# Latent attention: where the inverse sums are spread and the outputs scaled and split, in a two-layer transformer kernel

## The reference, cut to what matters

```python
for l in range(DEPTH):
    h = rms_norm(x, g_mix[l])
    proj = h @ w_in[l]
    c_q, c_kv, k_r, qkv_b, qkv_c, gate_logits = jnp.split(proj, IN_SPLITS, axis=-1)
    y_a = mla_mixer(c_q, c_kv, k_r, g_q[l], g_kv[l], w_uq[l], w_ukv[l])
    ...
    y_b = dilated_mixer(q_b, k_b, qkv_b[:, :, 2])
    y_c = neighbourhood_mixer(qkv_c[:, :, 0], qkv_c[:, :, 1], qkv_c[:, :, 2], rpb[l])
    ...
    merged = (gates[:, :, 0] * (y_a @ w_pa[l]) + gates[:, :, 1] * (y_b @ w_pb[l])
              + gates[:, :, 2] * (y_c @ w_pc[l]))
    x = x + merged @ w_o[l]
    ...

def attend(blk):        # in mla_mixer, 8 heads
    qn, qr = blk
    s = (jnp.einsum('bqhd,bkhd->bhqk', qn, k_nope) + jnp.einsum('bqhr,bkr->bhqk', qr, k_rope)) * scale
    p = jax.nn.softmax(s, axis=-1).astype(v.dtype)
    return jnp.einsum('bhqk,bkhd->bqhd', p, v)
```

## Time and profile before

| | before |
|---|---|
| median of 3 timed executions | 3363.31 us (3362.96 to 3364.73) |
| the profiled execution | 3372.84 us, its span 3371.0 us |
| TensorE busy (matmuls) | 3314.4 us, 98% |
| VectorE busy | 1596.5 us, 47% |
| ScalarE busy | 1244.7 us, 37% |
| GpSimd busy | 353.3 us, 10% |
| TensorE's share of the chain that ended last | 91% |

### The profile page before, as it was taken

The page is one execution under the profiler, slowest core; times in us unless marked ns, Lnnn a source line. Parts: engine busy times, 40 slices in busy tenths (PEclk is TensorE's granted clock), DMA queues, the critical chain, the costliest instruction groups (busy, mean ns, idle before and its releaser), DMA issues.

```text
span 3371.0 us, 39038 instructions
## 1 busy us (share of the span) xinstructions
PE 3314.4 (98%) x15780; PEld 2709.2 (80%) x15780; DVE 1596.5 (47%) x2314; ACT 1244.7 (37%) x2007; POOL 353.3 (10%) x321
## 2 busy tenths in 40 slices
PE   8999999999999999999999999999999999999998
PEld 7885788888887867888888877878888888888887
DVE  5465444443445573445343544334433349754244
ACT  4564323322335553224322332222322247742222
POOL 3121000100011220001000111002200032230001
PEclk9999999999999998999999999999999999999999
DMA  4121223222222211232222232222222222322222
GB/s 154 57 82 41 69 94 100 94 94 100 94 95 76 78 50 42 88 100 94 94 100 94 94 103 78 91 85 69 88 96 98 95 81 89 100 82 94 100 98 71
DMA packets 83234, 295.26 MB, mean 88 GB/s; under 512 B 9616, under 2 KB 12016, under 8 KB 82928
## 3 DMA queue, kind: packets, MB, share of 16 engines
q1 hardware_dynamic: 80352, 283.78, 25.4%
q0 software_dynamic: 2704, 8.98, 0.8%
HBM read 289.55 MB, written 3.18 MB: 87 GB/s over the span
## 4 chain that ended last, share of the span: by engine, by line
PE 91%; DVE 3%; ACT 2%; POOL 2%; issue 2%; DMA 0%; SPq 0%; DVEq 0%; ACTq 0%; POOLq 0%
PE bank L2504 27%; PE bank L2506 27%; PE bank L2505 27%; PE bank L2753 2%; PE bank L2761 2%; PE bank L2784 1%; PE bank L2896 1%; DVE w_lo L1872 1%; ACT w_hi L1420 1%; POOL xs L1210 1%; PE bank L2723 1%; PE bank L2585 1%; PE bank L2886 1%; PE bank L2646 0%; PE bank L2595 0%
## 5 line engine op out<-in xcount | busy, mean ns | idle before, releaser
L1872 DVE TENSOR_TENSOR w_lo<-raw_ring,w_hi 128x1024 fp32r<-128x1024 f32 x530 | 666.8, 1259 | 1155.8 <-ACT w_hi L1420 1155.1
L2504 PE MATMUL bank<-h_hi,w_hi 128*128 128x512 f32 (+1 forms) x2752 | 1065.5, 387 | 15.5 <-DVE w_lo L1872 10.6
L2506 PE MATMUL bank<-h_hi,w_lo 128*128 128x512 f32 (+1 forms) x2752 | 1054.6, 383 | 0.0
L2505 PE MATMUL bank<-h_lo,w_hi 128*128 128x512 f32 (+1 forms) x2752 | 1054.5, 383 | 0.0
L1420 ACT ACTIVATE w_hi<-raw_ring 128x1024 fp32r<-128x1024 f32 x530 | 560.6, 1058 | 1168.9 <-PE bank L2506 1095.8
L2504 PEld LDWEIGHTS bank<-h_hi,w_hi 128*128 128x128 f32 x2752 | 520.2, 189 | 120.2 <-issue 15.0
L2506 PEld LDWEIGHTS bank<-h_hi,w_lo 128*128 128x128 f32 x2752 | 519.6, 189 | 102.2
L2505 PEld LDWEIGHTS bank<-h_lo,w_hi 128*128 128x128 f32 x2752 | 520.3, 189 | 100.2 <-issue 1.5
L2504 PE MATMUL bank<-act_hi,w_hi 128*128 128x512 f32 (+1 forms) x1336 | 507.6, 380 | 2.1 <-ACT arena L1440 1.2
L2506 PE MATMUL bank<-act_hi,w_lo 128*128 128x512 f32 (+1 forms) x1336 | 504.7, 378 | 0.0
L2505 PE MATMUL bank<-act_lo,w_hi 128*128 128x512 f32 (+1 forms) x1336 | 504.5, 378 | 0.0
(11 more groups left out here) (211 smaller groups left out, 2652.0 us busy)
## 6 DMA issues: line engine op xcount, KB each, us to landing
raw_ring<-weights SPq DMA_DIRECT2D x530, 512.0 KB, 3.3
arena<-rpb POOLq DMA_DIRECT2D x16, 320.0 KB, 3.6
xs<-x_t SPq DMA_DIRECT2D x8, 256.0 KB, 6.5
out_t<-xs SPq DMA_DIRECT2D x16, 128.0 KB, 1.8
arena<-block SPq DMA_DIRECT2D x1, 1024.0 KB, 9.0
arena<-o_nat POOLq DMA_DIRECT2D x2, 512.0 KB, 3.4
arena<-ret POOLq DMA_DIRECT2D x4, 256.0 KB, 3.2
o_nat<-arena POOLq DMA_DIRECT2D x2, 384.0 KB, 3.1
```

Source lines behind the costliest of these rows:

```text
L1872: nc.vector.tensor_tensor(w_slot(w_lo, u), raw_slot(u), f32(w_slot(w_hi, u)), ALU.subtract) \
L2504: nc.tensor.matmul(out, lhs[0], rhs[0], start=first, stop=False)
L2505: nc.tensor.matmul(out, lhs[0], rhs[1], start=False, stop=False)
L2506: return nc.tensor.matmul(out, lhs[1], rhs[0], start=False, stop=last)
```

## The change

It does five things.

- The generator of a latent group yields R no longer together with O, but with four new kinds of step from a table, `LATENT_ENDS`: E (reciprocal and spread), R, Y (the multiplication) and H and L (high and low part of the split). E of the first output is in step j = 6 in place of 4, R in step 7; batch 0 of the next dense part holds Y of the first; batch 1 H of the first and E of the second; batch 2 L of the first and R of the second.
- Y, H and L of the second output come later still: for A0 in steps 1, 2 and 3 of A1's main part, behind that step's transposes (`LATENT_LAST`), for A1 behind projections 3, 4 and 5 of C1 (`LATENT_DENSE`). `turned` does nothing for A any more.
- V of a latent group asks `before` only for the units in which V's own weights lie (`units_of`), no more all that have a free slot. The others come with the pairs of heads (`split_ahead`).
- In the dense part of a group with rotation VectorE does `turned` ahead of the last weight split and the last rotation (B0 is the one group that this concerns).
- The plan of banks and the order of splits follow.

```diff
-TURNS = {("B", 0): [("C", 0)], ("A", 1): [("B", 2), ("A", 0)], ("C", 1): [("A", 1)]}
+TURNS = {("B", 0): [("C", 0)], ("A", 1): [("B", 2)]}
...
+LATENT_ENDS = {6: [("E", 3)], 7: [("R", 3)], 8: [("Y", 3)], 9: [("H", 3), ("E", 7)], 10: [("L", 3), ("R", 7)]}
+LATENT_LAST = {1: "Y", 2: "H", 3: "L"}
+LATENT_DENSE = {3: "Y", 4: "H", 5: "L"}
...
         if br == "A":
-            ends = j >= LATENT_LAG_O and ends_head(br, g, j - LATENT_LAG_O)
-            if ends:
+            if j >= LATENT_LAG_O and ends_head(br, g, j - LATENT_LAG_O):
                 yield "O", j - LATENT_LAG_O
             if LATENT_LAG_T <= j < n + LATENT_LAG_T:
                 yield "T", j - LATENT_LAG_T
-            if ends:
-                yield "R", j - LATENT_LAG_O
+            if g and part == "main" and j in LATENT_LAST:
+                yield LATENT_LAST[j], -1
+            if j in LATENT_ENDS:
+                yield from LATENT_ENDS[j]
             continue
...
+        def units_of(key):
+
+            return piece_at[weight_pieces(key)[-1]][0] + 1
...
+            def latent_end(l, kind, g, two):
+                if kind == "H":
+                    wait_freed(act, (l, "A", g, "O", two))
+                    hi((l, "yt", "A", g, two), part(act_hi, YT_TILE["A", g] + two), latent_out(two))
...
+                            key = (l, "v", br, g, t)
+                            if br == "A":
+                                before(key, units_of(key) - split[0])
...
+            def latent_end(l, kind, g, two):
+                y = latent_out(two)
+                if kind == "E":
+                    both = slice(2 * NT * two, 2 * NT * (two + 1))
+                    wait_freed(dve, (l, "A", g, "S", 2 * NT * (two + 1) - 1))
+                    then(nc.vector.reciprocal(row_inv[:, both], latent_sum[:, both]))
+                    if g:
+                        dve.wait_ge(lo_ready, lo_at[l, "yt", "A", 0, two])
+                    else:
+                        dve.wait_ge(mixed_b, l + 1)
+                    inv = row_inv[:, both].rearrange("p (s t o) -> p t s o", s=2, o=1)
+                    nc.vector.tensor_copy(y.rearrange("p (t s d) -> p t s d", t=NT, s=2),
+                                          inv.to_broadcast([P, NT, 2, HEAD])).then_inc(latent_inv, 1)
+                elif kind == "Y":
+                    key = (l, "A", g, "O", two)
+                    wait_acc(dve, key)
+                    wait_freed(dve, (l, "A", g, "R", two))
+                    nc.vector.tensor_tensor(y, bank(key)[:, :], y, ALU.mult).then_inc(latent_freed, 1)
+                elif kind == "L":
+                    i = YT_TILE["A", g] + two
+                    lo((l, "yt", "A", g, two), part(act_lo, i), y, part(act_hi, i))
...
+                        if (br, g) == ("C", 1) and m in LATENT_DENSE:
+                            latent_end(l, LATENT_DENSE[m], 1, 1)
...
+                    for group_ in TURNS.get((br, g), []):
+                        turned(l, group_)
                     if has_rope(br) and n_dense(br, g) == 5:
                         before((l, "v", br, g, 0))
                         rotate(l, br, g, 4)
-                    for group_ in TURNS.get((br, g), []):
-                        turned(l, group_)
```

More of the change, by code:

```diff
@@ L531, in turned @@
         def turned(group):
-            for f in range(0 if group[0] == "A" else 2):
+            for f in range(2):
                 p.add((l, "yt") + group + (f,), "dve")
@@ L550, in attend @@
                         p.add((l, "vt" if turns_v(br, g) else "v", br, g, t), "act")
+                    continue
+                if kind in "EYHL":
                     continue
@@ L664, in split_order @@
         out.extend((("h", "q", l, k), True) for k in range(2))
-        for br, g in GROUPS:
-            if (br, g) in YT_TILE:
-                out.extend(((l, "yt", br, g, f), br == "A") for f in range(2))
+        for br, g, f in SPLIT_TURNED:
+            out.append(((l, "yt", br, g, f), br == "A"))
         out.extend((("merged", l, m), True) for m in range(KD))
@@ L1593, in turned @@
                     key = (l, "yt") + group + (f,)
-                    if group[0] == "A":
-                        wait_freed(act, (l,) + group + ("O", f))
-                        hi(key, part(act_hi, YT_TILE[group] + f), latent_out(f))
-                        continue
                     before(key)
@@ L2149, in turned @@
             def turned(l, group_):
-                if group_[0] == "A":
-                    for two in range(2):
-                        key = (l,) + group_ + ("O", two)
-                        wait_acc(dve, key)
-                        wait_freed(dve, (l,) + group_ + ("R", two))
-                        y = latent_out(two)
-                        nc.vector.tensor_tensor(y, bank(key)[:, :], y, ALU.mult).then_inc(latent_freed, 1)
-                    for f in range(2):
-                        i = YT_TILE[group_] + f
-                        lo((l, "yt") + group_ + (f,), part(act_lo, i), latent_out(f), part(act_hi, i))
-                    return
                 for f in range(2):
@@ L2168, in attend @@
                     if kind == "V":
-                        if not turns_v(br, g):
+                        if br == "A":
+                            key = (l, "v", br, g, v_tiles(j)[-1])
+                            before(key, units_of(key) - split[0])
+                        elif not turns_v(br, g):
                             before((l, "v", br, g, v_tiles(j)[-1]))
+                        continue
+                    if kind in "EYHL":
+                        latent_end(l, kind, *latent_pair(g, j))
                         continue
@@ L2183, in attend @@
                             nc.vector.tensor_copy(pt_tile(br, u)[:, 0:w], b[:, 0:w]).then_inc(dve_freed, 1)
-                            if br == "A" and ends_head(br, g, j):
-                                both = slice((i - 1) * NT, (i + 1) * NT)
-                                then(nc.vector.reciprocal(row_inv[:, both], latent_sum[:, both]))
-                                if g:
-                                    dve.wait_ge(lo_ready, lo_at[l, "yt", "A", 0, j // NT])
-                                else:
-                                    dve.wait_ge(mixed_b, l + 1)
-                                inv = row_inv[:, both].rearrange("p (s t o) -> p t s o", s=2, o=1)
-                                nc.vector.tensor_copy(
-                                    latent_out(j // NT).rearrange("p (t s d) -> p t s d", t=NT, s=2),
-                                    inv.to_broadcast([P, NT, 2, HEAD])).then_inc(latent_inv, 1)
                         elif kind == "O" and ends_head(br, g, j):
```

16 lines of the change are left out of this document (13 added, 3 removed).

## The result

| | before | after |
|---|---|---|
| median of the timed executions | 3363.14 us (4, 3362.47 to 3364.73) | 3346.34 us (4, 3346.05 to 3346.63) |
| the profiled execution, its span | 3372.84 us, 3371.0 us | 3346.27 us, 3344.5 us |
| VectorE / ScalarE / GpSimd busy | 1596.5 / 1244.7 / 353.3 us | 1599.1 / 1242.6 / 355.9 us |

The ratio is 0.9949 with a 95% interval of 0.9932 to 0.9967. The forecast was 3345.3 us, so the total missed by 1.0 us. Its terms missed by more, in both directions. Two executions of the kernel before that ran beside the later experiments took 3696 and 3804 us, at a mean granted clock of 0.84 and 0.82; they are left out of all comparisons.

What follows compares the result with a forecast made beforehand. TensorE, busy almost throughout, was taken to be held up by waits for other engines. 2 x 0.4 + 12.05 + 3.4 + 1.7 = 17.95, say 18.0 us, off the 3363.31 us median gave 3345.3 us; 8-in-10 range 3335 to 3353.

Steps and rivals of the forecast that it cites:

- Part 1: A0: spread copy behind T5, its transpose behind T6, so TensorE no longer waits there; gain 2.0 us per layer.
- Part 2: A0: a weight split moved behind T1's copy collides with GpSimd's multiplication, making pair 3 late; loss 1.6 us per layer.
- Part 3: Start of A1: less VectorE work ahead of the first maxima; first scores to first output 15.05 us, gain 12.05 in sum.
- Part 4: Start of C1: one split instead of two multiplications and two splits before the first mask; 1.7 us per layer, sum 3.4.
- Part 5: B0: splitting C0's outputs ahead of the rotation removes TensorE's wait for V's banks; 0.87 us per layer, sum 1.7.
- from S3 on within 0.4 us of A0's timing: A1: following three engine queues pair by pair, from S3 on it nearly matches A0, giving 15.05 us to first output.
- rival (b): A1: VectorE and ScalarE don't keep up, half of the 12.05 us stays; 3351.3 us, chance 0.10.
- between the two: C1 should end between C0's 18.1 us and its own 20.2 in layer 0; 1.7 us per layer taken.
- Part 6: C1, layer 1: 9.5 us of slow clock belong to the profiled execution only, not the median, and will be absent after.
- Rival (a): C1, layer 1: the median holds the slow-clock stretch too and loses it; 9.5 us lower, 3335.8 us, chance 0.18.
- Rival (c): A1 and C1: waits only move into A1's dense part, leaving 2.5 us of gain; 3360.8 us, chance 0.06.
- Rival (d): A0, A1, C1: remaining waits bring on slow-clock stretches, 9.5 us apiece; with three 3373.8 us, chance 0.04.

Runs made afterwards that it cites:

- run without multiplications: The changed kernel without GpSimd's three multiplications of the dilated outputs by their weights, the two additions kept; 3350.61 us.
- the early split: The changed kernel with all of V's weight units in A0 split ahead of V again, as in the kernel before; 3343.05 us, ratio 0.9936.
- part 1 alone: The kernel before with only the first half's spread copy put behind pair 5's transposes and its transpose behind pair 6's; 3361.54 us, ratio 0.9996.
- part 3 half taken back: The changed kernel with A0's second output's multiplication and split, and both weight splits, again at the head of A1; 3354.45 us.

## Why the prediction was right, and where it was not

| part | predicted, us in all | measured |
|---|---|---|
| A0 (parts 1 and 2) | 0.8 | 2 x 0.29 = 0.6 |
| A1 (part 3) | 12.05 | 5.5 + 3.65 = 9.15 |
| C1 (part 4) | 3.4 | 2 x 2.0 = 4.0 |
| B0 (part 5) | 1.7 | 2 x 0.94 = 1.9 |
| sum | 17.95 | 15.6 |

The medians differ by 16.8 us. The other 1.2 us have no place in the groups; 0.3 of them are there before B0. Against the repeated profile of the kernel before (its span is 17.0 us longer than that of the changed kernel) the rest lies between the layers, 1.65 us that B0 doesn't explain, and there the clock over 1000 to 1020 us is 0.83 in one profile and 0.91 in the other. That is chance of the executions compared; for the medians it is not shown. So it is partly luck that the total missed by only 1.0 us: the terms were 2.4 us too high, and 1.2 us that no term names made up for half of it.

**Part 1** held: 2.02 us by TensorE's rows, and alone in the kernel before it gives the same.

**Part 2** held with its mechanism and its size: split 2.60 us (2.65 was implied), maxima of pair 3 11.72 us behind S0 instead of 9.74, so 2.0 us late for a forecast 2.2, loss 1.73 us where 1.6 was forecast. The run without multiplications moved the collision to an addition, and the early split took it away. What the prediction didn't say is that the two parts don't simply add. The sum 2.0 - 1.6 is right for the change as a whole, since it counts the loss with the spread copy already moved. But the loss of part 2 without part 1 is only 0.29 us, because GpSimd's end hides it, and part 1 on top of part 2 is worth 0.58 us, not 2.0. Whoever tried part 2 alone would have found it nearly free.

**Part 3** is the term that was mis-sized, by 2.9 us. The cause was right: with half of the work back in front, S0 to O0 rises by 2.65 us. The step that failed is "from S3 on within 0.4 us of A0's timing". The queues were followed up to the scores, and those are in time (S5 13.39 us after S0, in A0 before 13.07). But O0 needs T3's copy, and half of the copies are ScalarE's, behind the exponentials of the next pair. VectorE's maxima of pair 4, late by a weight split and an output split, reach O0 that way: 1.17 us in each layer. The booking of 13.6 of 14.9 us said that VectorE has the time on average, not that it has it ahead of pair 4. The other part of the miss is 0.2 to 0.3 us per layer over the whole stretch, and has no cause shown. This is rival (b) in its mechanism, at a quarter of the term and not at half. With VectorE's weight splits behind pair 4 the 15.05 us were met at 15.21. The difference between the layers, 1.7 us in layer 0 alone, was rightly taken as clock; the unchanged kernel's repetition shows it as one row of 3.62 us.

**Part 4** gave 2.0 us per layer for 1.7, inside its bounds of 1.1 to 2.1. The step that was mis-sized is "between the two": C1 comes within 0.15 us of C0's 18.10 in spite of the split in front. The clock has no share in the 2.0, although it went from 0.92 to 1.00: the stage takes 20.23 us at either (layer 0 before, and layer 1 with part 1 alone). It follows the first mask one to one, 1.99 us for a mask 1.99 us earlier, and 1.39 for 1.39 with the multiplication and the high part back in front. Only the last 0.6 us are worth less, 0.25.

**Part 5** was right: 0.94 for 0.87, just above its bound (1.9 us in all for 1.8), and the wait returns when the order does.

**Part 6** was the riskiest choice, since its 9.5 us were over half of the gain, and it held. Rival (a) is excluded by the repetition, whose span is 9.5 us shorter with the same program. Rival (c) is excluded by A1 and C1. Rival (d), that the new wait of T3 brings on stretches at half clock, did not come: A0, A1 and C1 run at 1.00 in the changed kernel. It is not without ground, though. In the run without multiplications T3's wait of 1.8 us was followed by 1.8 us of scores at double length, and so were 1.9 us waits in A1, in one layer or both, of the kernel before, with part 1 alone or without, and of the one with part 3 half taken back. The 1.31 us wait was not followed by it in either layer.

## What to carry to other kernels

When work moves from the head of a group into the gaps between its steps, follow every consumer to the engine that copies for it. An average of free time says nothing on the queue in front of one maximum. Put VectorE's operations with two inputs in SBUF where GpSimd rests, and where two late engines hide one another, cost the parts in both orders. Before the difference between a profile and a median is explained, profile the same kernel once more.

## What was not expected of the hardware

The lock between VectorE and GpSimd works both ways. The split beside an addition took 3.05 us instead of 1.23, and the addition behind it 3.21 instead of 2.35.

A wait of TensorE of 1.8 to 1.9 us in the latent groups was followed, in some layers and executions and not in others, by four score matmuls at half clock, wholly or in part (2.84 to 3.65 us instead of 1.88 to 1.96). After 1.31 us it was not seen. What it costs depends on its place. Behind T0 in A1 and T3 in A0 it cost 1.4 to 1.7 us from S0 to O0. On the second scores of A1 it cost nothing once (20.19 us at 0.92, 20.20 at 1.00). Behind C1's wait of 1.52 us a mean clock of 0.92 cost nothing (20.23 us, as at 1.00), one of 0.84 cost 1.2 us (21.47). In one execution of the kernel before, and in no other profile, the stretch behind that same wait of 1.52 us lasted over 20 us. What decides between none, a short and a long stretch stays open.
